# Recurrence of one prompt block and of the samples: from a stage of its own into the beats of the expert stage

## The reference, cut to what matters

```python
def trunk_layer(x, ...):
    h = rmsnorm(x, norm1_g)
    p = h @ w_in                                    # conv 512 | rwkv 1408 | attention 1152 columns
    y_conv, conv_new = conv_mixer(p_conv, ...)
    y_rwkv, shift_new, wkv_new = rwkv_mixer(p_rwkv, shift_prev, wkv_state, ...)
    y_att = sb_attention(q, k_all, v_all, past_len, att_bias).reshape(B, T, ATT_DIM)
    mix = jnp.concatenate([y_conv, y_rwkv, y_att], axis=-1)
    x = x + mix @ w_out
    h2 = rmsnorm(x, norm2_g)
    x = x + peer(h2.reshape(B * T, D), ...)          # 16 of 16384 experts per head, 8 heads
    return x, (k, v, conv_new, shift_new, wkv_new)

def _wkv_step(S, inp):                               # the recurrence of rwkv_mixer, per token, 6 heads of 64
    r, w, k, v, kk, b = inp
    sa = jnp.einsum('bhvk,bhk->bhv', S, kk)
    S = S * w[:, :, None, :] - sa[..., None] * b[:, :, None, :] + v[..., None] * k[:, :, None, :]
    return S, jnp.einsum('bhvk,bhk->bhv', S, r)
...
    ym = jnp.mean(y, axis=-1, keepdims=True)         # then, per head
    yn = (y - ym) * lax.rsqrt(yv + GN_EPS) * ln_g + ln_b
    out = (yn + bonus) * g

def peer_block(xb, w_query, sub_keys, u_tab, v_tab):
    s = ...                                          # scores against 2 x 128 keys, per head
    top_s, pos = lax.top_k(cand_s, PEER_TOPK)        # 16 experts e of 16 x 16 candidates
    act = jax.nn.gelu(jnp.einsum('thkd,td->thk', u_tab[e], xb))
    return jnp.einsum('thk,thkd->td', gate * act, v_tab[e])
```

## Time and profile before

| | us |
|---|---|
| launches, median of 3 (lowest, highest) | 3707.83 (3703.47, 3716.29) |
| the profiled execution: first to last instruction | 3701.2 |
| of it the front (to the first expert's dot product) | 714.1 |
| of it the expert stage | 2987.1 |
| busy in the profiled execution: PE, DVE, ACT, POOL | 2819.3 (76%), 2586.4 (70%), 1458.7 (39%), 1345.8 (36%) |
| moved by DMA | 1258.48 MB |

### The profile page before, as it was taken

One profiled execution on the slowest core, in us unless ns is written; L12 is line 12 of the kernel. 1 busy time (PEld: TensorE's weight loads), 2 busy tenths in 40 slices (PEclk: granted clock), 3 DMA queues, 4 the chain that ended last, 5 costly groups with the idle time before them and its releaser, 6 DMA issues.

```text
span 3701.2 us, 52809 instructions
## 1 busy us (share of the span) xinstructions
PE 2819.3 (76%) x19164; PEld 1380.3 (37%) x19164; DVE 2586.4 (70%) x6424; ACT 1458.7 (39%) x2994; POOL 1345.8 (36%) x1205
## 2 busy tenths in 40 slices
...
DMA  3113404599999999999999999999999999999998
GB/s 95 36 54 89 145 2 141 206 386 406 382 410 414 412 391 408 410 403 381 408 413 406 383 393 407 401 378 410 401 416 376 399 416 416 406 412 413 411 418 345
DMA packets 248982, 1258.48 MB, mean 340 GB/s; under 512 B 57673, under 2 KB 84593, under 8 KB 113041
## 3 DMA queue, kind: packets, MB, share of 16 engines
...
...
## 4 chain that ended last, share of the span: by engine, by line
DMA 26%; PE 24%; DVE 18%; ACT 9%; issue 5%; POOL 1%; DVEq 0%; SPq 0%; ACTq 0%; POOLq 0%
DMA uv_first<-in_peer_uv,expert 13%; PE peer_y L2282 12%; DMA uv_rows<-in_peer_uv,expert 11%; PE peer_s L1972 5%; DVE uv_first L1749 4%; DVE uv_rows L1749 3%; ACT diag L1947 2%; ACT L1939 2%; PE beside L2001 2%; DMA w_out_rows<-in_w_out 2%; PE scan L2075 2%; ACT L1887 2%; DVE weights L1476 1%; DVE same L1452 1%; DVE same L1454 1%
## 5 line engine op out<-in xcount | busy, mean ns | idle before, releaser
L1408 POOL DMA_INDIRECT uv_first<-in_peer_uv,expert x604 | 691.0, 1144 | 1111.1 <-PE peer_y L2282 815.1
L2282 PE MATMUL peer_y<-uv_first,diag 64*64 64x512 f32 x4688 | 753.6, 757 | 421.7 <-ACT diag L1947 409.6
L1749 DVE CUSTOM_DVE_ANT_0 uv_first<-uv_first,p_h 128x1024 f32<-128x1024 f32 x604 | 729.1, 1223 | 225.4 <-DMA uv_first<-in_peer_uv,expert 223.4
L2282 PE MATMUL peer_y<-uv_rows,diag 64*64 64x512 f32 x3504 | 566.8, 757 | 296.9 <-ACT diag L1947 289.9
L1408 POOL DMA_INDIRECT uv_rows<-in_peer_uv,expert x452 | 509.1, 1126 | 670.2 <-PE peer_y L2282 589.7
L1749 DVE CUSTOM_DVE_ANT_0 uv_rows<-uv_rows,p_h 128x1024 f32<-128x1024 f32 x452 | 546.4, 1222 | 154.2 <-DMA uv_rows<-in_peer_uv,expert 152.8
L1939 ACT ACTIVATE gelu<-hidden 128x2 f32<-128x2 f32 x528 | 107.3, 203 | 1123.2 <-DVE hidden L1749 1116.7
L1947 ACT ACTIVATE diag<-p_ident,weights 128x128 f32<-128x128 f32 x1024 | 355.1, 394 | 484.3 <-DVE weights L1476 480.4
L2282 PEld LDWEIGHTS peer_y<-uv_first,diag 64*64 64x64 f32 x4688 | 184.1, 159 | 785.4 <-ACT diag L1947 568.7
L2282 PEld LDWEIGHTS peer_y<-uv_rows,diag 64*64 64x64 f32 x3504 | 136.7, 159 | 563.3 <-ACT diag L1947 410.2
L591 PE MATMUL proj<-mix,w_in_tile 128*128 128x512 f32 x672 | 296.8, 600 | 0.0
...
## 6 DMA issues: line engine op xcount, KB each, us to landing
...
```

Source lines behind the costliest of these rows:

```text
L1408: pool.indirect_dma_start(out=uv(m, ALL, slice(0, 2 * D)), out_offset=None, in_=io["peer_uv"], in_offset=bass.IndirectOffsetOnAxis(ap=expe ...
L1749: nc.vector.tensor_tensor_reduce(out=uv(m, ALL, slice(0, D)), in0=uv(m, ALL, slice(0, D)), in1=h2[:, b % 2, :], scale=1.0, scalar=0.0, op0 ...
L2282: ins = nc.tensor.matmul(Y[r][rows[j], :], diag[rows[r], m % (2 * GP), rows[r]], uv(m, rows[r], slice(D + j * 512, D + (j + 1) * 512)), st ...
```

## The change

`FRONT` becomes 1. `scan_rwkv` keeps one double chunk (block 0) and nothing of the samples; its loops over turns are written out. `finish_rwkv` handles block 0 alone, all three pairs of heads in one go; the rest of it (gates, key products) stays. The block's rows go to a scratch of their own, `mixed_first`, and are loaded in the prelude; `mixed` and `mixed_sample` hold convolution rows only. The closing product takes the recurrent rows from the tile in which `finish` left them (`ykept`).

In the expert stage `scan` in block `b` now serves block `b + 1`, the one that closes in the same block. So close, sample and late attention start 16 beats later; the scan starts at beats 2 and 19. Block 7 gets `scan_sample`, the samples' chunk, in 26 beats from beat 4, and `finish` from beat 31; its state lies in the buffer of `w_out`. Sample sequence `b` is handled in block `b`. Since `h2t` is ready at beat 53, the scores and selections of the next block's first two heads come after it: groups 6 of turn 6 and 1 and 5 of turn 7 (scores), all eight groups of turn 7 (selection); turn 6 has no selection. SP's queue is reordered.

```diff
-FRONT = 2
+FRONT = 1
+LATER = NBLK - 1 - FRONT
...
# project
-                        later = slice(FRONT * P, SEQ)
+                        later = slice(FRONT * P, SC)
...
-            sp.dma_start(io["mixed_sample"][:, 0:CT, :], cy[:, :, SEQ:T]).then_inc(conv_out, 16)
+            sp.dma_start(io["mixed_sample"], cy[:, :, SEQ:T]).then_inc(conv_out, 16)
...
# scan_rwkv
-        def turns(eng, turn):
-
-            turn(0, *prompt_sets, (0, 1), True, False)
-            for c in range(1, TURNS):
-                turn(c, *prompt_sets, (0, 1), False, False)
-            turn(0, *sample_sets, (0,), False, True)
...
             sp.dma_start(eye[:, :], io["eye2"]).then_inc(const_in, 16)
-            sp.dma_start(masks[:, :, :, :], io["chunk_masks"]).then_inc(const_in, 16)
-            sp.dma_start(s0[:, :, :, :], io["state_wkv"]).then_inc(const_in, 16)
-            sp.dma_start(tmask[:, :, :], io["seq_mask"]).then_inc(const_in, 16)
+            sp.dma_start(masks[:, :, :], io["scan_masks"]).then_inc(const_in, 16)
...
-            sp.wait_ge(S2, 2 * PR)
-            sp.dma_start(io["wkv_new_sample"], s0[:, :, :, :]).then_inc(SO, 16)
-            sp.wait_ge(SO, 16)
+            sp.wait_ge(const_in, 32)
...
# finish_rwkv, PE
+            E.did(nc.tensor.matmul(b1[:, :, :], m[:, :], y, start=True, stop=True), "mean")
+            pe.wait_ge(const_in, 16)
+            pe.wait_ge(sig, 1)
+            gate(0)
+            pe.wait_ge(A.sem, A.at("sq"))
+            E.did(nc.tensor.matmul(b3[:, :, :], m[:, :], sq[:, :, :], start=True, stop=True), "var")
+            for n in beside(0):
+                key_product(nc, pe, sb, bk, n)
+            for i in range(1, PR):
+                gate(i)
+            for n in range(6, WK_EARLY):
                 key_product(nc, pe, sb, bk, n)
...
# peer
-    CLOSE, X, SPREAD, H2, TURN, H2T = 24, 33, 34, 35, 35, 37
-    EARLY, LATE, BEATS = 5, 38, 64
-    SCAN, FINISH = (2, 20), 36
+    CLOSE, X, SPREAD, H2, TURN, H2T = 40, 49, 50, 51, 51, 53
+    EARLY, LATE, BEATS = 21, 54, 64
+    SCAN, FINISH = (2, 19), 35
+    S_SCAN, S_FINISH = 4, 31
...
+    scored = lambda t, q: {(PH - 2, 6): t + 2, (PH - 1, 1): t + 2, (PH - 1, 5): t + 3}.get((t % PH, q), t + 3 if q == 1 and t % PH < PH - 3 else TURNS)
+    kept = lambda t, q: {(PH - 2, 7): t + 2, (PH - 1, 2): t + 2, (PH - 1, 7): t + 3}.get((t % PH, q), t + 3 if q == 7 and t % PH < PH - 3 else TURNS)
+    chosen = lambda t, q: {PH - 2: (TURNS, 0), PH - 1: (t + 1 + q // 4, q % 4)}.get(t % PH, (t + 2, q // 2) if q % 2 else (TURNS, 0))
+    exped = lambda t, q: {(PH - 1, 3): t + 1, (PH - 1, 7): t + 2}.get((t % PH, q), t + 2 if q == 7 and t % PH < PH - 2 else TURNS)
+    gated = lambda t, q: {(PH - 1, 0): TURNS, (PH - 1, 4): t + 1}.get((t % PH, q), t + 1 if q == 0 else TURNS)
...
# beats
                 if n - FINISH in range(5):
                     finish(scanned(b), n - FINISH)
+            else:
+                if n - S_SCAN in range(S_STEPS):
+                    scan_sample(n - S_SCAN)
+                if n - S_FINISH in range(5):
+                    finish(ATTENDED, n - S_FINISH)
...
-            if early_seq(b) is not None:
-                sample(early_seq(b), n - EARLY)
-            if late_seq(b) is not None:
-                sample(late_seq(b), n - LATE)
+            sample(b, n - EARLY)
...
# SP
+            def scan_load_sample():
+
+                sp.wait_ge(FV.sem, FV.at("gated", LATER - 1))
+                sp.dma_start(xin[:, :, :], io["scan_in"][LATER * CPB]).then_inc(state_in, 16)
+                sp.dma_start(smask[:, :, :], io["scan_masks_sample"]).then_inc(state_in, 16)
+                sp.wait_ge(wo_used, ATTENDED * DC)
+                sp.dma_start(s0, io["state_wkv"]).then_inc(state_in, 16)
...
+            sp.dma_start(ykept[:, :, :], io["mixed_first"]).then_inc(first_in, 16)
...
                 if not last(b):
                     residual(b + 1)
-                    if scanned(b) is not None:
-                        scan_load(scanned(b), 1)
+                if scanned(b) is not None:
+                    scan_load(scanned(b), 1)
+                    scan_load(scanned(b), CPB)
+                if sample_turn:
+                    sp.wait_ge(ACT_S.sem, ACT_S.at("y"))
+                    sp.wait_ge(PE_S.sem, PE_S.at(f"out{PR - 1}"))
+                    sp.dma_start(fin[:, :, :, 0:CH], io["finish_in"][LATER][:, :, :, 0:CH]).then_inc(xin_in, 16)
+                    sp.wait_ge(DVE_S.sem, DVE_S.at(f"out{PR - 1}"))
+                    sp.dma_start(io["wkv_new_sample"], s0).then_inc(state_out, 16)
+                    sp.wait_ge(state_out, 16)
+                    weights(b + 1, 0)
+                    weights(b + 1, 1)
+                if not last(b):
                     for c in range(2, DC):
                         weights(b + 1, c)
-                if scanned(b) is not None:
-                    scan_load(scanned(b), CPB)
+                if b + 1 < ATTENDED:
+                    if scanned(b + 1) is not None:
+                        scan_load(scanned(b + 1), 0)
+                    else:
+                        scan_load_sample()
                 if late_att(b) is not None:
                     attention(late_att(b))
-                if scanned(b) is not None:
-                    sp.wait_ge(FV.sem, FV.at("gated", b))
-                    sp.dma_start(io["mixed"][scanned(b)][:, CT:CT + PR, :], ykept[:, :, :]).then_inc(mixed_out, 16)
...
# DVE
-                    if q == 0 and t + 1 < TURNS:
-                        gates(t + 1)
-                    if t + LEAD < TURNS:
-                        for piece in range(4 * q // GROUPS, 4 * (q + 1) // GROUPS):
-                            choose(t + LEAD, piece)
+                    if gated(t, q) < TURNS:
+                        gates(gated(t, q))
+                    later_turn, piece = chosen(t, q)
+                    if later_turn < TURNS:
+                        choose(later_turn, piece)
...
# PE, close_y
+                if c == CT:
+                    if b:
+                        pe.wait_ge(FV.sem, FV.at("gated", b - FRONT))
+                    else:
+                        pe.wait_ge(first_in, 16)
+                recurrent = s_mixed if last(b) else ykept
+                left = mixb[:, c, :] if c < CT else recurrent[:, c - CT, :] if c < CT + PR else att[:, c - (CT + PR), :]
```

865 lines of the change are left out of this document (475 added, 390 removed).

## The result

The changed kernel takes 3755.9 us (median of 4, 3750.6 to 3764.5) against 3705.7 us (median of 4): a ratio of 1.0125, 95% interval 1.0101 to 1.0149. It is slower by 50 us; the ratio is estimated on its own and is not the quotient of the two medians (1.0135). I had said 3693, with 3736 as the upper end of the range.

What follows compares the result with a forecast made beforehand. The expert stage was taken as bound by DMA of gathered rows, except in attention turns. Front -107 and expert stage +92 on the 3701.2 us span gave 3686; with medians 6.6 above the span, 3693 us, range 3632 to 3736.

Steps and rivals of the forecast that it cites:

- Front: Stages ahead of the expert stage: scan stage ends after one double chunk, finish stage shorter; -107 us, bounds -102 and -110.
- (a): Turn 7 of blocks 0 to 5: two selections beside the first four attention units, 48.5 to 58 us each, +57 us.
- (b): Turn 0 of blocks 3 to 6: second attention units meet `add_values`, first scan steps and final norm; 51.5 us each, +22.
- portions: Third attention portions in blocks 5 and 6 and the half portion in block 2: +8 us, bounds 0 and 12.
- (c): Slow turns carry about 0.6 MB less, as sample's pages and output weights go to other turns: +9 us in six blocks.
- (d): Old turn 3 of blocks 1 to 5: the close leaves the scan, a gain of 14 us, bounds -5 and -20.
- (f): Samples' recurrence in block 7: its PE burst falls into one group, +4 us; with the bytes +6.
- (e): Turn 7 of blocks 6 and 7: two selections without attention, +4 us, bounds 0 to 6.
- Number 3: Turns 0 and 1, blocks 3 to 6: PE's queue holds back attention's products and buffers; +41 us, 3734; chance 0.23.
- the prediction's signs: Expected in the profile, among others: turn 3 under 46 us; blocks 0 to 5 longer by 9 to 18 us each.

Runs made afterwards that it cites:

- e5: The kernel before with the new selection order alone (none in turn 6, two in turn 7): 3723.9 us, ratio 1.0054 to the kernel before.
- e2: The changed kernel with the second head's selection spread over the two turns ahead of it: 3762.9 us, ratio 1.0150 to the kernel before.
- e3: The changed kernel with the final norm moved from turn 0 to turn 2 and the second chunk's load ahead of the output store: 3733.4 us.
- e1b: The changed kernel with unneeded filler work (fills) on DVE, ACT or PE in nine turns, read for times alone: 3744.9 us, a single run.
- e11: The changed kernel with only the scores moved behind the beat's other work on PE: 3737.3 us, ratio 1.0089 to the kernel before.
- e4: The changed kernel with the second chunk's steps and the finish one beat later: 3734.6 us, ratio 1.0072 to the kernel before.
- v1: The kernel before with only the samples' chunk moved from the front to blocks 6 and 7 of the expert stage: 3643.0 us, ratio 0.9827.

## Why the prediction was wrong

**Front**, right in its total: -107.9 us against -107, and the expert stage began at 606.2. That it is right to a microsecond is luck: the finish stage began at 489.1 and not at 486.6, because `project` ended later, for which I had no term, and the finish stage and the prelude, shorter by 1.4 and 1.9 us more than I had, made up for it.

**(a)** right: turn 7 of blocks 0 to 5 against the old turn 5 makes +54 us (sum of six differences) for 57; the short groups hold most of it, and e5, e2 and the DVE fill confirm that the price is that of work on DVE in a turn that DVE's chain paces.

**(b)** is the step that failed. I gave turn 0 of blocks 3 to 6 the cost of one engine's additions, a value between two engines' totals: "If all adds up on DVE it is 53.4, by ACT at the same 94% it is 50.7; I take 51.5". Measured were 56.9 to 58.2 us, +45 for the four (231.2 against 186.0) where I had 22. The overlap that I assumed between the two engines' additions is not there. I had 7.5 us for DVE (a wait of 1.5 in it) and 4.6 for ACT; their sum put on 45.9 is 58.0. By busy time DVE got 5.9 and ACT 5.5 us in block 4, 11.4 together, for a turn that grew by 12.1. In an attention turn each group's gelu waits for DVE's dot products, DVE's weights for the gelu, ACT's exponential for DVE's subtraction, so the two engines work by turns and an addition to the engine whose turn it is lengthens the round. e3 shows it for one addition, the norm (2.6 of 2.8 us paid in block 4), the groups' timelines for the others. It is no rule for every addition: in e1b, 5.1 us more on DVE cost turn 0 only 1.4 and 2.6 more on ACT nothing. That the busy shares (ACT 94% of the old turn 6) hid this, since ACT was at work there because it was nearly always its turn, is my reading. Turn 1 of blocks 4 to 6 and turns 0 of blocks 1 and 2, for which I had 8 us of portions, cost 27, I think for the same reason; no run tries them alone.

**No term at all** had the scores ahead of the recurrence. I wrote down that the scan starts "at beats 2 and 19" and costed nothing for the one beat; e11 measures 13 to 19 us for the scores' place (14 in turn 4), and e4 about 20 for the beat, in which the finish moves as well. I had followed the moved DMAs past everything in SP's and POOL's queues, but not the moved products past what PE's program holds in the same group.

**(c), (d), (f).** (d), the close leaving the scan, was near: old turns 3 of blocks 1 to 5 sum to 239.0 us, new turns 5 to 229.0, -10 for my -14. (e) +7 for 4. (f) was half its size: block 7 without turn 7 is longer by 12 us, and v1 shows 18.7 for the same work in blocks 6 and 7. (c) can't be separated. 54 + 45 + 27 + 7 - 10 + 12 = 135 of the 169 us. Of the remaining 34 the scores' place is 13 to 19; (c), for which I had 9, and what is unnamed make the other 15 to 21, and their cause stays open.

**The rivals.** Number 3 had the place and nearly the times (turn 0 at 58, turn 1 at 54; measured 58 and up to 52), but by PE's queue. The fills show PE as one link of the chain, not the one that holds the buffers: 7.7 us of PE work cost 2 us, and of the 2.7 us in group 3 of turn 0 the wait for PE is 1.1 and the masks on DVE the rest. My chance of 0.23 for it was too low, and that its price over mine (+41) is close to (b)'s miss (23 + 19) is a coincidence of sizes, since its mechanism was another; it gave 3734, and what lies above that and above the range is of the size of the scores' 13 to 19 us. Two of the prediction's signs failed as well: turn 3 was not under 46 us, and blocks 0 to 5 were longer by 11 to 24 us, not 9 to 18.
